# Eight down blocks of the last feed-forward stage as seven products, and the convolution's first tap on ScalarE

## The reference

```
h2 = rmsnorm(x, norm2_w)
a, v = jnp.split(h2 @ ffn_w_up, 2, axis=-1)
a = jax.nn.gelu(causal_dwconv(a, ffn_conv_w, ffn_conv_b), approximate=False)
return x + (a * v) @ ffn_w_down
```

## Time and profile before

| | us |
|---|---|
| median of three runs | 1402.67 |
| span of the profiled execution | 1401.5 |
| PE busy | 1394.9 |
| DVE busy | 1097.5 |
| ACT busy | 859.1 |
| POOL busy | 226.2 |
| last feed-forward stage, blocks 2 to 21 and the end | 1226.0 to 1401.5 |

### The profile page before, as it was taken

One profiled execution on the slowest core, in us unless ns is written; L12 is line 12 of the kernel. 1 busy time (PEld: TensorE's weight loads), 2 busy tenths in 40 slices (PEclk: granted clock), 3 DMA queues, 4 the chain that ended last, 5 costly groups with the idle time before them and its releaser, 6 DMA issues.

```text
span 1401.5 us, 20322 instructions
## 1 busy us (share of the span) xinstructions
PE 1394.9 (100%) x7680; PEld 1195.7 (85%) x7680; DVE 1097.5 (78%) x1665; ACT 859.1 (61%) x1393; POOL 226.2 (16%) x309
## 2 busy tenths in 40 slices
PE   9999999999999999999999999999999999999999
PEld 7888888898888888888888988888887899888887
DVE  7878878776978878788787778788777877688776
ACT  6657655855667657676557646666567765455553
POOL 1112123000111001112050001114149200100000
PEclk9999999999999999999999999999999999999999
DMA  9999755465999859998455458999547336456551
GB/s 369 300 299 281 217 182 182 138 199 187 300 256 291 210 183 306 273 280 221 171 197 178 165 181 271 272 275 261 190 146 254 123 121 221 156 175 216 194 183 58
DMA packets 86330, 304.28 MB, mean 217 GB/s; under 512 B 11724, under 2 KB 11864, under 8 KB 86232
## 3 DMA queue, kind: packets, MB, share of 16 engines
q1 hardware_dynamic: 72120, 251.84, 51.2%
q0 software_dynamic: 13824, 50.34, 18.9%
q10 hardware_dynamic: 288, 0.79, 0.1%
HBM read 301.87 MB, written 1.06 MB: 216 GB/s over the span
## 4 chain that ended last, share of the span: by engine, by line
PE 97%; ACT 1%; DMA 1%; DVE 0%; issue 0%; POOL 0%; ACTq 0%; POOLq 0%
PE bank L747 18%; PE bank L754 9%; PE bank L701 9%; PE bank L702 9%; PE bank L703 9%; PE bank L926 5%; PE bank L925 5%; PE bank L929 5%; PE bank L731 3%; PE bank L768 3%; PE bank L738 3%; PE bank L773 3%; PE bank L732 3%; PE bank L769 3%; PE bank L721 1%; PE bank L1025 1%
## 5 line engine op out<-in xcount | busy, mean ns | idle before, releaser
L1971 DVE TENSOR_TENSOR wlo<-raw,whi 128x1024 fp32r<-128x1024 f32 x409 | 491.7, 1229 | 13.3 <-ACT whi L1364 13.2
L1364 ACT ACTIVATE whi<-raw 128x1024 fp32r<-128x1024 f32 x409 | 417.8, 1049 | 21.8 <-PE bank L703 14.2
L747 PE MATMUL bank<-hx,whi 128*128 128x512 f32 x1088 | 268.5, 393 | 0.0
L747 PEld LDWEIGHTS bank<-hx,whi 128*128 128x128 f32 x1088 | 200.5, 188 | 41.3 <-issue 2.0
L701 PE MATMUL bank<-whi,hid 128*128 128x512 f32 x536 | 211.1, 394 | 0.0
L702 PE MATMUL bank<-wlo,hid 128*128 128x512 f32 x536 | 209.2, 390 | 0.0
L703 PE MATMUL bank<-whi,hid 128*128 128x512 f32 x536 | 208.8, 389 | 0.0
L754 PEld LDWEIGHTS bank<-hx,wlo 128*128 128x128 f32 x1088 | 142.9, 191 | 7.6
L754 PE MATMUL bank<-hx,wlo 128*128 128x256 f32 x1088 | 145.2, 282 | 0.0
L1971 DVE TENSOR_TENSOR wlo<-gates,whi 128x1024 fp32r<-128x1024 f32 x96 | 116.0, 1220 | 6.6 <-ACT whi L1364 6.0
L703 PEld LDWEIGHTS bank<-whi,hid 128*128 128x128 f32 x536 | 100.6, 188 | 21.4
(11 more groups left out here) (297 smaller groups left out, 2420.1 us busy)
## 6 DMA issues: line engine op xcount, KB each, us to landing
raw<-w_dram SPq DMA_DIRECT2D x414, 512.0 KB, 4.6
gates<-w_dram POOLq DMA_DIRECT2D x64, 512.0 KB, 7.8
gates<-w_dram SPq DMA_DIRECT2D x32, 512.0 KB, 5.0
arena<-w_dram POOLq DMA_DIRECT2D x32, 512.0 KB, 8.8
arena<-w_dram SPq DMA_DIRECT2D x16, 512.0 KB, 5.3
gain<-g_dram SPq DMA_DIRECT2D x7, 512.0 KB, 3.3
out_dram<-x SPq DMA_DIRECT2D x4, 256.0 KB, 2.5
par<-p_dram SPq DMA_DIRECT2D x1, 867.0 KB, 10.1
```

Source lines behind the costliest of these rows:

```text
L747: e.matmul(b[:, :], hi_of(j)[:, k * P:k * P + P], hx[:, k * 2 * S:k * 2 * S + 2 * S], start=k == 0, stop=False, skip_group_check=True)
L1364: e.activation(hi_of(t), raw_of(t), ACT.Copy).then_inc(sem["w_hi"], 1)
L1971: e.tensor_tensor(lo_of(t), raw_of(t), hi_of(t).bitcast(F32), ALU.subtract).then_inc(sem["w_lo"], 1)
```

## The change

The stage's order becomes a written list, `MORDER`, that all engines follow: `N` is a block, `d` a down block, `z`/`y` a quarter product of one octet half, `Q` the same product for both, `f` an addition of weight quarters, `h` and `s` the splitting of hidden values, `o` an output.

- The down blocks of features 8 to 15 go. Blocks 8 to 11 (z) and 12 to 15 (y) are taken in pairs. For each pair the left matrix has two block columns (the two blocks) and two block rows (the halves of the tokens), the right one two block rows and two block columns (the halves of the 1024 columns). The 2 x 2 product is made of seven products instead of eight. Each product runs over the z tile and the y tile, two pairs in each.
- The products of these blocks stay as plain float32 in wide buffers (`hfo`, 1024 columns). ACT makes the high part, POOL the low part, four sums or differences in place (256 columns each), then again a high part (ACT) and a low part (POOL).
- The weight tiles for products 4 to 7 are sums of quarters. SP loads four tiles at once for z (in the place of tile a8) and four for y (a13); POOL adds them (three additions of 1024 columns for each) and issues one accumulating transfer for each.
- Products 2, 3 and 4 accumulate straight into the side banks; 1, 5, 6 and 7 get banks of the ring, and DVE adds them to `x` in eight operations with the right signs.
- The first of the convolution's three operations moves from DVE to ACT, as an activation with a scale and a bias; gelu(0) moves behind the second transposed block.
- The last block is computed in the same order as the others. The counters of POOL's memsets become one.

```diff
+QSLOT = {5: 0, 7: 1, 6: 2, 4: 3}
+OCTET = range(8, 16)
+MORDER = """N2 N3 d0 N4 d1 N5 d2 N6 d3 N7 d4 N8 d5 N9 N10 d6 fz5 N11 fz6 N12 fz4 hz N13 fy5 d7 z2 N14 sz fy6 z4 N15 z3 fy4 N16 hy N17 d16 y2
+            N18 sy y4 Q1 o1 N19 y3 d17 Q6 o6 N20 Q5 o5 N21 Q7 o7""".split()
...
+            def load_quarters(u, slot):
+                for i, q in enumerate(("11", "12", "11", "21")):
+                    off = addends["Mf", u, q]
+                    e.dma_start(slot(i), wstream[off * P:(off + TW) * P].rearrange("(p n) -> p n", p=P)).then_inc(sem["ld_q"], 16)
...
+                if j == T["Mfa8"]:
+                    E.wait_ge("ft", K.FT["Mf", 1])
+                    load_quarters("z", qform_z)
+                if j == T["Mfa13"]:
+                    E.wait_ge("qf", 1)
+                    load_quarters("y", qform_y)
...
+            def quad(s, n, parts="z"):
+                tag = STAGES[s]
+                ring = n in (1, 5, 6, 7)
+                b = claim((tag, "q", n)) if ring else side[{2: 0, 3: 1, 4: 2}[n]]
+                at = {1: 0, 6: 0, 7: 1, 2: 2, 3: 2, 4: 3, 5: 3}[n]
+                for u in parts:
+                    j = T[f"{tag}{u}{n}"]
+                    own = octet[u]
+                    whole = n in (1, 2, 4)
+                    hi, lo = own[0:2] if whole else own[2:4]
+                    E.wait_ge("qs", 6 * PARTS(u) + (1 if whole else 6))
+                    wait_tile(j)
+                    for p in range(2):
+                        col = (4 * p + at) * P
+                        ins = mm3(b[:, :], hi[:, col:col + P], lo[:, col:col + P], hi_of(j)[:, p * 512:p * 512 + 512], lo_of(j)[:, p * 512:p * 512 + 512],
+                                  p == 0 and ring and u == parts[0], p == 1 and ring and u == parts[-1])
+                    ins.then_inc(sem["tile"], 1)
...
-                    if 3 < i < NF - 1:
+                    if i > 3:
                         ba, bb = claim((tag, "a", i)), claim((tag, "b", i))
...
-                        accum(s, i - 3)
...
+                def first_tap(i):
+                    if i < 2:
+                        E.wait_ge("pad", i + 1)
+                    else:
+                        E.wait_ge("sum", K.SUMV[s, i] + 1)
+                        E.wait_ge("act", K.MULV[s, i - 2])
+                    e.activation(cvb[i % 2], pads[i % 4][:, 2:258], ACT.Identity, bias=PR("fbias")[:, i:i + 1],
+                                 scale=PR("fw")[:, 3 * i + 2:3 * i + 3]).then_inc(sem["cv1"], 1)
...
+                    if w[0] == "h":
+                        E.wait_ge("mul", K.MULV[s, OCTET[{"z": 3, "y": 7}[w[1]]]])
+                        e.activation(octet[w[1]][0], hfo[w[1]], ACT.Copy).then_inc(sem["hf"], 3)
+                    if w[0] == "s":
+                        E.wait_ge("qs", 6 * PARTS(w[1]) + 5)
+                        e.activation(octet[w[1]][2], hfo[w[1]], ACT.Copy).then_inc(sem["hf"], 1)
...
                 def conv(i):
                     ap, cv = pads[i % 4], cvb[i % 2]
...
-                    e.tensor_scalar(cv, ap[:, 2:258], fw[:, 3 * i + 2:3 * i + 3], fb[:, i:i + 1], ALU.mult, ALU.add).then_inc(sem["cv"], 1)
-                    E.wait_ge("cv", 3 * i + 1)
+                    E.wait_ge("cv1", i + 1)
...
+                    if i in OCTET:
+                        u, q = "zy"[i // 4 % 2], i % 4
+                        e.tensor_tensor(hfo[u][:, q * S:q * S + S], sl[:, :], up, ALU.mult).then_inc(sem["mul"], 1)
+                        return
...
+            def quad_form(n, u):
...
+                if n == 5:
+                    E.wait_ge("ld_q", 64 * k + 64)
+                    e.tensor_tensor(slot(0), slot(0), slot(1), ALU.add).then_inc(sem["qf"], 1)
...
+                    e.dma_start(slot(1), wstream[off * P:(off + TW) * P].rearrange("(p n) -> p n", p=P), accum_op=ALU.add).then_inc(sem["add_q"], 16)
+                if n == 6:
+                    E.wait_ge("add_q", 16 * k + 16)
+                    e.tensor_tensor(slot(2), slot(2), slot(1), ALU.add).then_inc(sem["qf"], 1)
...
+            def quad_low(k, done, dst, src, high):
+                E.wait_ge("hf", 4 * k + done)
+                e.tensor_tensor(dst, src, high.bitcast(F32), ALU.subtract).then_inc(sem["qs"], 1)
+
+            def quad_sums(k, buf):
+                k0 = 6 * k + 1
+                a11, a21, a12, a22 = (quad_part(buf, i) for i in range(4))
+                E.wait_ge("qs", k0)
+                e.tensor_tensor(a22, a22, a21, ALU.subtract).then_inc(sem["qs"], 1)
...
+            def last_ffn():
+                for w in MORDER:
...
+                    if w[0] == "h":
+                        quad_low(k, 3, lo, buf, hi)
+                        quad_sums(k, buf)
+                    if w[0] == "s":
+                        quad_low(k, 4, lo2, buf, hi2)
+                    if w[0] == "f":
+                        quad_form(int(w[2]), u)
```

More of the change, by code:

```diff
@@ L211, in form_of @@
         return FORMS[int(name[6])]
+    if name[-2] == "z" and int(name[-1]) in QSLOT:
+        return "Q", QSLOT[int(name[-1])]
+    if name[-2] == "y" and name[-1] in "4567":
+        return "R", QSLOT[int(name[-1])]
     return None, 0
@@ L223, in addend_layout @@
                     off += TW
+    for u in "zy":
+        for q in ("11", "12", "21", "22"):
+            at["Mf", u, q] = off
+            off += TW
     return at, off
@@ L362, in banks @@
                     continue
-                for i in range(2, NF):
+                for w in MORDER:
+                    if w in ("Q1", "Q5", "Q6", "Q7"):
+                        claim((tag, "q", int(w[1])), *(("q_ev", 1) if w == "Q1" else ("qx", QX[tag][{6: "v", 7: "w", 5: "r22"}[int(w[1])]])))
+                    if w[0] != "N":
+                        continue
+                    i = int(w[1:])
                     claim((tag, "a", i), "sum", self.SUMV[st, i] + 1)
@@ L1392, in hidden_hi @@
                     E.wait_ge("tile", DONE[K.HIDTILE[h_ - 4]])
-                e.activation(hid[h_ % 4][:, 0:S], src, ACT.Copy).then_inc(sem["hidhi"], 1)
+                e.activation(hid[h_ % 4][:, 0:S], src, ACT.Copy).then_inc(sem["hidhi"], hid_step(h_))
             def sil_of(s, i):
@@ L1546, in from_tokens @@
                     E.wait_ge("ft", K.FT[tag, i])
-                    E.wait_ge("padz", 4)
+                    E.wait_ge("zero", 19)
                     e.activation(pads[i][:, 2:258], bank[K.BANK[tag, "ft", i][0]][:, 0:S], ACT.Copy).then_inc(sem["pad"], 1)
                 def hidden(i):
+                    if i in OCTET:
+                        return
                     E.wait_ge("mul", K.MULV[s, i])
                     hidden_hi(K.HID0[s] + i, prod[(K.MUL0[s] + i) % 2][:, :])
-                for i in range(2, NF):
+                for w in MORDER:
+                    if w[0] == "d":
+                        ahead(T[f"{tag}{w}"])
+                    if w[0] in "zyQ":
+                        for u in "zy" if w[0] == "Q" else w[0]:
+                            ahead(T[f"{tag}{u}{w[1]}"])
+                    if w[0] == "h":
[4 more added lines that the diff above has]
+                        e.activation(octet[w[1]][2], hfo[w[1]], ACT.Copy).then_inc(sem["hf"], 1)
+                    if w == "o1":
+                        E.wait_ge("tile", DONE[f"{tag}y1"])
+                        e.activation(qcf, bank[K.BANK[tag, "q", 1][0]][:, :], ACT.Copy).then_inc(sem["q_ev"], 1)
+                    if w[0] != "N":
+                        continue
+                    i = int(w[1:])
                     ja, jb = T[f"{tag}a{i}"], T[f"{tag}b{i}"]
@@ L1570, in ffn @@
                         hidden(1)
+                    first_tap(i)
                     gelu(i)
@@ new lines, in last_ffn @@
+            def last_ffn():
+                for w in MORDER:
+                    if w[0] in "zyQ" or w[0] not in "hsf":
+                        continue
+                    u = w[1]
+                    k, (hi, lo, hi2, lo2), buf = PARTS(u), octet[u], hfo[u]
+                    if w[0] == "h":
[5 more added lines that the diff above has]
+                        quad_form(int(w[2]), u)
@@ L2774, in mixer2 @@
                 for i in (0, 1, 3):
-                    e.memset(rows[i][:, :], 0.0).then_inc(sem["rowz"], 1)
+                    e.memset(rows[i][:, :], 0.0).then_inc(sem["zero"], 1)
                 def q_rstd(a):
@@ L2914, in tail, with quad @@
             src[f"{tag}wo{i}"] = lambda i=i: wo[i * P:(i + 1) * P]
+    def quad(tag, u, wd, blocks):
+        part = lambda r, q: np.concatenate([wd[blocks[2 * p + r] * P:(blocks[2 * p + r] + 1) * P, q * 512:q * 512 + 512] for p in range(2)], 1)
+        for n, r, q in ((1, 0, 0), (2, 1, 0), (3, 1, 1)):
+            src[f"{tag}{u}{n}"] = lambda r=r, q=q: part(r, q)
+        for r in range(2):
+            for q in range(2):
+                quarters[tag, u, f"{r + 1}{q + 1}"] = part(r, q)
     def group(tag, w):
```

190 lines of the change are left out of this document (140 added, 50 removed).

## The result

The changed kernel takes 1415.0 us (1414.5 to 1415.4, 5 runs) against 1402.8 (1402.7 to 1404.9, 5 runs) of the kernel before beside it: a ratio of 1.0083, 95% interval [1.007, 1.0095]. It is slower by 0.8%; 1411.0 was forecast, in a range to 1417.

The account below looks back on a forecast made before the run. PE was taken to bound the kernel as long as DVE stays ahead. 1402.7 - 2.7 (fewer matmuls) + 11.1 (PE waiting for DVE, held by POOL) = 1411.1, taken as 1411.0 us; range 1399.8 to 1417.

Parts of the forecast that it names:

- PE's part: Last feed-forward stage on PE: 96 matmuls removed, 84 added at 0.228 us each, so PE gets 2.7 us less.
- The rival of another pace: The seven products' matmuls on PE: at 0.24 us each the gain is 1.8, not 2.7; no chance of its own.
- POOL beside DVE: From block 12's end: POOL's two-input SBUF operations take turns with DVE's, bank readers do not wait; 19.8 us of hold.
- The wide hold: One 1024-column POOL operation beside DVE: holds the port for 2.2 us, with ends of 0.6 and 2.9 us.
- How much of the hold reaches DVE: DVE's list from block 12's end: three quarters of it is blocked by POOL's hold, 14.9 us.
- The stall: PE behind block 12: DVE's list of 73.8 us plus 14.9 exceeds the 77.6 available, so PE waits 11.1 us.
- z's forms "free": POOL's three form operations for z around blocks 5 to 7: need only loads, banks come free 8 us early; free.
- The tap: Convolution's first tap on ACT: about 0.4 us there, DVE waits about 0.5 us per block; costed at nothing.
- From the span to the time: Whole kernel: the median of the runs lies 1.2 us above the profiled span of 1401.5, taken to stay.
- Memory: nothing: Weight loads of the stage: sixteen 512 KB transfers for eight, 4.2 MB more, covered by splitting five tiles ahead; costs nothing.
- DVE stays ahead: Last stage: POOL's operations fall into DVE's idle time and sums, so PE never waits; 1400.0 us, chance 0.22.

Follow-up runs that it names:

- best1: Changed kernel with weight sums by accumulating DMAs, hidden values' low parts and sums on DVE, and an order that fills DVE's waits: 1400.2 us.
- forms_dma: Changed kernel with the six additions of weight quarters made by accumulating DMAs in place of POOL's 1024-column additions: 1409.3 us.
- tap_only: Kernel before with only the convolution's first tap moved to ACT and gelu(0) behind the second transposes: 1403.2 us.
- tap_back: Changed kernel with the convolution's first tap back on DVE: 1415.6 us.
- best2: Changed kernel with weight sums by accumulating DMAs and an order that fills DVE's waits; hidden values' low parts and sums stay on POOL: 1400.3 us.
- dve_lows: Changed kernel with the hidden values' low parts and sums on DVE; POOL keeps the six weight additions: 1414.8 us.
- splits_narrow: Changed kernel with DVE's splits of the eight summed quarter tiles cut from 1024 to 8 columns: 1410.1 us.
- fills_only: Changed kernel with the order alone altered, so that ready splits and other work fill DVE's waits; POOL's operations stay: 1405.1 us.
- dve_lows_dma: Changed kernel with weight sums by accumulating DMAs and hidden values' low parts and sums on DVE; POOL computes nothing in the stage: 1408.4 us.
- pool_narrow: Changed kernel with POOL's tensor operations of the last stage cut to 8 columns, waits and counters kept: 1404.5 us.
- pool_memset: Changed kernel with each of POOL's tensor operations of the last stage replaced by two memsets of the same tile, which read nothing: 1404.3 us.

## Why the prediction was right, and where not

The mechanism, the sign and the size were right; several terms were not.

- **PE's part, -2.7 us.** Right. The new products keep the pitch of the earlier trace rows (0.227), and best1, with no pause, is 2.9 us under before. The rival of another pace is out:

```profile
1316.50 0.39 PE L760 MATMUL bank<-whi,quads 128*128 128x512 f32 x1
1316.73 0.39 PE L761 MATMUL bank<-wlo,quads 128*128 128x512 f32 x1
```

- **POOL beside DVE.** The rule read from operations of 256 columns holds at 1024: turns between two of DVE's, and bank readers do not wait (413 ns above, as the earlier trace rows had it). The Trainium skill (SBUF — State Buffer, "SBUF: two separate sides") has it that the pair is locked for a whole instruction, and only against a GpSimd operation that reads SBUF; both halves of that are borne out, by 6.74 us for two splits and by the memsets' 1218 ns. The wide hold is 2.4 to 2.5 us, not 2.2; with a wait for DVE 2.9 to 3.4.
- **How much of the hold reaches DVE.** Forecast: three quarters of 19.8, 14.9 us. Measured as what DVE's operations took beyond their usual time: splits 58 x 0.163 = 9.5, low parts 14 x 0.244 = 3.4, multiplications 3.5, convolutions 2.1: 18.5 us, of which 5.3 by z's forms ahead of block 12. So 13.2 where 14.9 stood.
- **The stall.** Forecast 11.1 us behind block 12; there 12.3 - 1.4 = 10.9 us. That is closer than the terms deserve, and partly luck: the hold was 1.7 us smaller and the wait for the tap 1.5 us larger. Of the places forecast, z4 and z3, block 17, d16 and y2, d19 and d20 have pauses, d19 the longest with 2.4 us. d21 has none, and y3, y6 and d18 (1.6 us together) were not forecast.
- **z's forms "free": the step that failed.** I argued from the banks of PE, which come free early, and did not look where DVE stands. Already in the kernel before DVE is behind at the stage's head: block 4's `a` product was done at PE by 1245.4, and DVE summed it at 1251.29, having idled for only 0.76 and 0.48 us between. It has caught up only by 1287, where it idles 0.93 us for the bank copy:

```profile
1249.02 2.35 DVE L1971 TENSOR_TENSOR wlo<-raw,whi 128x1024 fp32r<-128x1024 f32 x2
1251.29 0.42 DVE L2170 TENSOR_TENSOR arena<-arena,bank 128x256 f32<-128x256 f32 x1
...
1287.44 0.42 DVE L2170 TENSOR_TENSOR arena<-arena,bank 128x256 f32<-128x256 f32 x1 [0.93 <-ACT arena L1538]
```

  z's forms fell in between, each on an operation of the hidden path (after):

```profile
1262.00 2.18 DVE L2127 TENSOR_TENSOR hid<-prod,hid 128x256 fp32r<-128x256 f32 x1 [0.48 <-ACT hid L1482]
...
1267.45 0.48 DVE L2306 SCALAR_TENSOR_TENSOR arena<-arena,par 128x256 f32<-128x256 f32 x1 [0.67 <-ACT arena L1635]
...
1270.06 2.27 DVE L2328 TENSOR_TENSOR prod<-sil,prod 128x256 f32<-128x256 f32 x1
1272.81 2.07 DVE L2127 TENSOR_TENSOR hid<-prod,hid 128x256 fp32r<-128x256 f32 x1 [0.48 <-ACT hid L1482]
```

  They cost d5's 1.4 us directly, and in forms_dma, with y's, 5.7 in all.
- **The tap.** It takes 0.60 us on ScalarE, not 0.42 (I priced it by the gelu), and DVE waits 0.67, not 0.5. Over nine blocks that is 1.5 us of DVE's list. "Nearly nothing is won" was right by tap_only and tap_back.
- **No term for the clock and the restarts.** A pause was priced at its length. It cost 0.08 us more each (0.9), and the one at d19 another 1.4 by the clock. With d5's 1.4 that makes 3.7 us. The forecast was short by 3.3 us in the span (1409.8 against 1413.1), which is these 3.7 less the 0.2 by which the stall was too large and the 0.3 by which the sum above overshoots.
- **From the span to the time.** The other 0.7 of the 4.0 us by which 1411.0 was short is the distance between the two, taken as 1.2 us. It is 1.9 (1415.0 and 1413.1), and was no less before: an execution with a span of 1401.5 took 1403.29. The 1.2 set one execution's span against a median of three.
- **Memory: nothing,** as costed. In the stage after, no wait of DVE, ACT or PE is put down to a transfer.
- **The rival "DVE stays ahead", 1400.0,** gave the time that the seven products allow once nothing makes PE pause: best1 and best2 are there. But against it stood one thing more than POOL. At the list's end DVE has d19's and d20's splits behind a wait and a block's sums, so POOL's turns gone leave 1404.4. This is that end after, where the splits of 1396.18 free d19:

```profile
1394.18 0.41 DVE L2314 TENSOR_TENSOR arena<-arena,bank 128x256 f32<-128x256 f32 x1
1395.26 0.48 DVE L2306 SCALAR_TENSOR_TENSOR arena<-arena,par 128x256 f32<-128x256 f32 x1 [0.67 <-ACT arena L1635]
1395.78 0.48 DVE L2308 SCALAR_TENSOR_TENSOR arena<-arena,par 128x256 f32<-128x256 f32 x1
1396.18 2.35 DVE L2091 TENSOR_TENSOR wlo<-raw,whi 128x1024 fp32r<-128x1024 f32 x2
```

dve_lows is 1.3 us above its range. In its profiled execution the pauses came to 10.2 us, their restarts to 0.7, and the clock fell twice, after 2.85 us of pause at 1313 and after d19's 2.36 (1.7 and 1.4 us). Added to 1401.5 - 2.7 that makes 1412.8 of its span of 1414.1 us; the rest is there before the stage, which it entered 1.4 us later than the kernel before (first transposes at 1230.16 against 1228.79). Left open: what makes executions come into the stage at different times (1228.3 to 1230.5 in the profiled ones, the latest with a fall of the clock ahead of the stage), and what decides whether the clock falls (next section but one).

## What to carry to other kernels

When work moves to an engine that is idle, ask what it reads and whose operations wait while it does (their rows are longer than usual beside it), and set its time against the list of that engine, stage by stage and from where that list stands at the time, not against the idle share of its own. An engine that is "95% full" by a sum with waits in it may have the air it needs inside those waits: put ready work in front of them before you call the engine the limit. A saving on the bounding engine shows only once nothing makes it pause, and a pause costs more than its length.

## What the runs showed that I had not expected

- The clock fell to half after some pauses of PE and not after others of the same length. It fell after 1.95 us in splits_narrow, 2.11 in fills_only, 2.18 at d19 in tap_back, 2.36 to 2.37 at d19 in four kernels (forms_dma, dve_lows, dve_lows_dma and the changed kernel, whose windows stand at 0.63 and 0.51) and 2.85 in dve_lows. It did not after 2.02 and 2.03 in pool_narrow and pool_memset, after 2.12 and 2.36 in tap_back, nor after 2.32 at d16 in the changed kernel itself, where products went on at 0.23. Where it fell, it cost 1.4 to 1.7 us.
- The same wait can be followed by a fall in one execution and by none in another. In pool_narrow the clock fell at 1077, long before the stage, after a wait of 1.33 us (windows at 0.94, 0.50 and 0.71); the kernel before has the same wait there, 1.35 us, and stays at 1.00. Its executions, too, fall into two groups: about four in five take 1402.2 to 1403.7 us, all at a mean clock of 1.00, the others 1404.4 to 1405.2, most of them at 0.998 or 0.999. What decides it is not settled.
- An order that only fills waits recovered 10 us with the contention still there, as much as taking the contention away (10.5).
- POOL's memsets of 128x1024 (0.96 us) leave DVE's reading operations untouched.
